# Moving the matmul operands' start addresses by 32, 96 and 128 bytes against the weights' in a two-layer hybrid trunk

## Chip, cores and metric

The kernel runs on one core of one Trainium2 chip. The metric is the device time of one execution in microseconds (us); lower is better. "Before" is the median of three runs.

## What is computed

Two residual layers over 512 tokens of width 1024, all in float32. Cut to what matters:

```python
for layer in range(2):
    xn = rmsnorm(h, norm_mix_g[layer])
    if layer % 2 == 0:      # S5 group + mLSTM group: one input projection, one output projection
        mix = s5_mlstm_mixer(xn, w_in, ..., w_q, w_k, ..., w_glu, w_out)
    else:                   # 16 query heads, 2 key/value heads, window 128
        mix = swa_sink_attention(xn, w_qkv, b_qkv, sinks, w_o, bias_band)
    h = h + mix
    gate, val = split(rmsnorm(h, norm_ffn_g[layer]) @ w_up)          # 1024 -> 2 x 2816
    h = h + (silu(causal_dwconv(gate, conv_w, conv_b)) * val) @ w_down   # 2816 -> 1024
return rmsnorm(h, norm_final_g)
```

## The kernel before

**Products.** Activations lie transposed: 128 channels on the partitions, the 512 tokens along the free dimension. A matmul's moving operand is one such block, 128 x 512, which is 2048 bytes in each partition; its stationary operand is a 128 x 128 block of weights, 512 bytes in each partition. Every float32 product is split into a high and a low part that are both float32r, and `block3` makes it of three matmuls: `whi` times the operand's high part (L1596), `whi` times its low part (L1597), `wlo` times its high part (L1598). Each of them has its own weight load.

**Weights.** SyncE streams the weights in tiles of 128 x 1024 through two buffers `raw`. ScalarE copies a tile to `whi` (L702), VectorE subtracts it to get `wlo` (L1057). Both are rings of 4 tiles of 4096 bytes, so that a weight block lies at a multiple of 512 bytes behind the start of `whi`.

**Operands.** Four pairs of tensors are the moving operands of the split products:

- `xhi`, `xlo`: the normed residual stream. Input projections, the feed-forward up projections (`product`), q/k/v of the attention, the S5 gate and the mixer's output projection.
- `ahi`, `alo`: 22 blocks of the gated feed-forward activation, used by the down projection (`down`). In layer 1 the last output tile is computed in two halves of 256 tokens.
- `xchi`, `xclo`: 4 blocks, from which q and k of the mLSTM are made (8 `block3`).
- `ohi`, `olo`: 8 blocks of the attention's output, used by its output projection (`wo_block`).

**Where they lie.** Offsets are per partition. `start_at(phase)` moves the next allocation up to a given phase in a line of `LINE` = 2048 bytes. `raw`, `whi`, `wlo`, `xhi`, `xlo` lie one behind the other and all start at phase 0. Behind them come constants (`con`, with the identity matrix; `mean_r`; `rstd`; `sq`; `ssum`; the parameters `prm`), and then, at `base`, a region that three layouts share, one after the other in time: the feed-forward's (`ahi`, `alo`, `gpad`, `cbuf`, `sbuf`, `vbuf`, `abuf`), the mixer's (`ff`, `gg`, `qT`, `kT`, `uc`, `uperm`, `xchi`, `xclo`, `sigo`, ...; `xin`, the input as loaded, lies in it too) and the attention's (`aq`, ..., `ohi`, `olo`, `st`). `plan` lays each out from `base`, sizes rounded up to 64 bytes, and moves `ohi` to `O_PHASE`. `A_PHASE` sets the phase of `base`. Up to `xchi` the mixer's layout has 65536 bytes, so `xchi` has the phase of `base`. `xc_at` is the same place as `xchi`, for tensors that take its room later: `m1re`, `m1im`, `vtok`, and behind `vtok` the buffer `wbuf` at `past_v` = `xc_at` + 8256. `h` lies at the end of the memory. With all phases 0, every moving operand of a `block3` starts at a multiple of 2048 bytes and every weight block at a multiple of 512.

**Other matmuls named below.** L1808 multiplies `vtok` (moving, 129 columns; a block lies 516 bytes behind the one before) with `wbuf` (stationary, slices of 512 bytes); it is in plain float32, of which the profile shows two instructions for each matmul. `qT` and `kT` are the operands of the mLSTM's scores (L1743), in plain float32 too.

Of the kernel before, what the change touches and what calls it, by code (L numbers as in the profile page):

```python
# [52 lines left out]
T_END = T_DN[1] + 3 * KB  # L53
assert T_WO + KB == T_UP[1] and T_END % 2 == 1

LINE, W_PHASE, X_PHASE, A_PHASE, O_PHASE = 2048, 0, 0, 0, 0
O_IN, O_O, O_GLU, O_OUT = 0, 12, 16, 20
O_UP = [28, 98]
O_DN = [O_UP[0] + 2 * FJ, O_UP[1] + 2 * FJ]
# [66 lines left out]
def build(nc, wstream, xT, params, bc, consts, band, outT, u_scratch):  # L126
# [9 lines left out]
    def at(name, shape, offset, dt=f32):  # L136
        return nc.alloc_sbuf_tensor_at(name, shape, dt, offset=offset)

    def size(shape):
        return (int(np.prod(shape[1:])) * 4 + 63) // 64 * 64  # L140
# [45 lines left out]
    def plan(*items, start=base):  # L186

        o, out = start, []
        for name, shape, dt in items:
            if name == "ohi":  # L190
                o += (O_PHASE - o) % LINE
            out.append(at(name, shape, o, dt))
            o += size(shape)
        assert o <= end, (items[0][0], o - end)
        return out


    h_at = end - size([P, KB, SEQ]) - (end - size([P, KB, SEQ])) % 64
    h = at("h", [P, KB, SEQ], h_at)
    ahi, alo, gpad, cbuf, sbuf, vbuf, abuf = plan(  # L200
        ("ahi", [P, FJ, SEQ], f32r), ("alo", [P, FJ, SEQ], f32r), ("gpad", [P, 2 + SEQ], f32),
        ("cbuf", [P, SEQ], f32), ("sbuf", [P, SEQ], f32), ("vbuf", [P, SEQ], f32), ("abuf", [P, SEQ], f32))
    assert base + 2 * size([P, FJ, SEQ]) + 5 * 2112 <= h_at

    F2 = [P, PAIRS, P]
    F4 = [P, 2, PAIRS, P]
    (ff, gg, qT, kT, uc, uperm, xchi, xclo, sigo, xs, ksb) = plan(
        ("ff", F4, f32), ("gg", F4, f32), ("qT", [P, HEADS, SEQ], f32), ("kT", [P, HEADS, SEQ], f32),
        ("uc", [P, GROUPS, NCH], f32), ("uperm", [P, 4, SEQ], f32),
# [2 lines left out]
    gg_at = base + size(F4)  # L212
    m1_at = base + 2 * size(F4)
    v_at = m1_at + 3 * 8192
    xc_at = v_at + 8192
    sigo_at = xc_at + 2 * 8192
    toep = at("toep", [P, CH, GROUPS, GCH], gg_at)
    gtmp = at("gtmp", [P, 2, PAIRS, GCH], base)
# [21 lines left out]

    tail = sigo_at + 8192 + size([P, 2, PAIRS, NCH]) + 2048
    bcp, xpad, cacc, xcf, ptmp, sm, qq, acol, turn, floor, hsm, selr = plan(
        ("bcp", [P, 4, PAIRS * GCH], f32), ("xpad", [P, 3 + SEQ], f32), ("cacc", [P, SEQ], f32),
        ("xcf", [P, SEQ], f32), ("ptmp", [P, 4, 256], f32), ("sm", [P, 40, PAIRS], f32),
# [1908 lines left out]
```

## Time and profile before

| | |
|---|---|
| median of three runs | 1069.69 us (1069.47 to 1070.51) |
| profiled execution | 1070.5 us, of it 1068.7 us span |
| granted TensorE clock | 0.998 of full speed, mean over the span |
| TensorE matmul busy | 1058.3 us (99%), 5552 instructions |
| TensorE weight load busy | 866.8 us (81%) |
| VectorE, ScalarE, GpSimd busy | 632.3 (59%), 464.6 (43%), 186.3 us (17%) |
| DMA | 107.27 MB, 29% of 16 engines' span |

The span goes from the first to the last instruction. The duration that the profile gives a matmul is from its start to its modelled end and overlaps the next one, so what a matmul costs in a dense stream is read from start to start, not from its duration.

### The profile page before, as it was taken

How to read it: one execution, taken by the hardware profiler on the slowest of the kernel's cores; microseconds unless marked ns; L12 is line 12 of the kernel's file. 1: busy time of each engine (PE TensorE's matmuls, PEld its weight loads, DVE VectorE, ACT ScalarE, POOL GpSimd, SP SyncE). 2: the span in 40 equal slices, each digit the busy share in tenths (PEclk: the TensorE clock that was granted, in tenths of full speed). 3: DMA queues.
4: the chain of work that ended last, by engine and by line, in shares of the span. 5: the costliest groups of instructions: out<-in, count | busy, mean ns of one | idle time of the engine just before them, and what ended most of it. 6: DMA issues, size and time to landing. Idle time of an engine off the chain costs nothing.

```text
span 1068.7 us, 15530 instructions
## 1 busy us (share of the span) xinstructions
PE 1058.3 (99%) x5552; PEld 866.8 (81%) x5552; DVE 632.3 (59%) x876; ACT 464.6 (43%) x733; POOL 186.3 (17%) x245
## 2 busy tenths in 40 slices
PE   9999999999999999999999999999999999999997
PEld 8787778888888888888888777888888888888886
DVE  6798755567666666633334774756666666643332
ACT  5455664544344444422323665554444444422221
POOL 8998911300000000000000221310000000000000
PEclk9999999999999999999999999999999999999999
DMA  6551025133222222323224111322222222222322
GB/s 231 168 128 40 15 91 197 59 119 118 94 89 92 98 98 98 98 99 118 98 102 144 61 60 41 118 94 100 85 99 93 98 98 98 98 99 99 119 79 79
DMA packets 36459, 107.27 MB, mean 100 GB/s; under 512 B 7808, under 2 KB 10112, under 8 KB 36160
## 3 DMA queue, kind: packets, MB, share of 16 engines
q1 hardware_dynamic: 36416, 106.69, 29.2%
q8 instruction: 28, 0.46, 0.2%
q14 instruction: 15, 0.12, 0.0%
HBM read 102.09 MB, written 3.15 MB: 98 GB/s over the span
## 4 chain that ended last, share of the span: by engine, by line
PE 93%; DVE 3%; ACT 1%; DMA 1%; SPq 1%; issue 1%; POOL 0%; DVEq 0%; ACTq 0%
PE bank L1596 29%; PE bank L1597 29%; PE bank L1598 29%; PE bank L1620 2%; DMA raw<-wstream 1%; PE bank L1986 1%; PE bank L1963 1%; PE bank L1743 1%; PE bank L1808 1%; DVE ssum L1090 0%; SPq L360 0%; PE bank L1707 0%; DVE wlo L1057 0%; DVE gtmp L1109 0%; PE bank L1687 0%
## 5 line engine op out<-in xcount | busy, mean ns | idle before, releaser
L1596 PE MATMUL bank<-xhi,whi 128*128 128x512 f32 x960 | 376.1, 392 | 0.8 <-DVE wlo L1057 0.6
L1597 PE MATMUL bank<-xlo,whi 128*128 128x512 f32 x960 | 373.7, 389 | 0.0
L1598 PE MATMUL bank<-xhi,wlo 128*128 128x512 f32 x960 | 373.6, 389 | 0.0
L1057 DVE TENSOR_TENSOR wlo<-raw,whi 128x1024 fp32r<-128x1024 f32 x177 | 226.0, 1278 | 205.4 <-ACT whi L702 204.8
L702 ACT ACTIVATE whi<-raw 128x1024 fp32r<-128x1024 f32 x177 | 187.1, 1058 | 323.2 <-PE bank L1598 301.0
L1596 PEld LDWEIGHTS bank<-xhi,whi 128*128 128x128 f32 x960 | 180.2, 188 | 40.6 <-DVE wlo L1057 1.0
L1598 PEld LDWEIGHTS bank<-xhi,wlo 128*128 128x128 f32 x960 | 180.2, 188 | 37.4
L1597 PEld LDWEIGHTS bank<-xlo,whi 128*128 128x128 f32 x960 | 180.3, 188 | 37.0 <-issue 0.2
L1596 PE MATMUL bank<-ahi,whi 128*128 128x512 f32 (+1 forms) x374 | 141.0, 377 | 0.0
L1598 PE MATMUL bank<-ahi,wlo 128*128 128x512 f32 (+1 forms) x374 | 140.8, 377 | 0.0
L1597 PE MATMUL bank<-alo,whi 128*128 128x512 f32 (+1 forms) x374 | 140.8, 377 | 0.0
L473 POOL COPY ssum<-sq 128x512 f32<-128x512 f32 x4 | 2.5, 614 | 554.9 <-ACT sq L708 554.9
L1596 PEld LDWEIGHTS bank<-ahi,whi 128*128 128x128 f32 x374 | 70.4, 188 | 13.0
L1598 PEld LDWEIGHTS bank<-ahi,wlo 128*128 128x128 f32 x374 | 70.4, 188 | 13.0
L1597 PEld LDWEIGHTS bank<-alo,whi 128*128 128x128 f32 x374 | 70.4, 188 | 12.7
L476 POOL TENSOR_TENSOR ssum<-ssum,sq 128x512 f32<-128x512 f32 x27 | 40.0, 1480 | 210.5 <-ACT sq L708 210.5
L973 ACT ACTIVATE ahi<-abuf 128x512 f32 x44 | 27.8, 632 | 72.5 <-DVE abuf L1430 72.5
L1432 DVE TENSOR_TENSOR alo<-abuf,ahi 128x512 f32 x44 | 30.5, 693 | 41.1 <-ACT ahi L973 41.1
L708 ACT ACTIVATE sq<-h 128x512 f32<-128x512 f32 (+1 forms) x31 | 19.4, 625 | 75.3 <-DVE h L1445 63.9
L1419 DVE SCALAR_TENSOR_TENSOR cbuf<-gpad,prm,cbuf 128x512 f32<-128x512 f32 x44 | 33.1, 752 | 6.7 <-DVE cbuf L1417 6.7
L1422 DVE SCALAR_TENSOR_TENSOR cbuf<-gpad,prm,cbuf 128x512 f32<-128x512 f32 x44 | 33.1, 752 | 6.7 <-DVE cbuf L1419 6.7
L1430 DVE TENSOR_TENSOR abuf<-vbuf,sbuf 128x512 f32<-128x512 f32 x44 | 30.5, 693 | 5.4
(264 smaller groups left out, 1052.1 us busy)
## 6 DMA issues: line engine op xcount, KB each, us to landing
raw<-wstream SPq DMA_DIRECT2D x177, 512.0 KB, 3.2
xin<-xT SPq DMA_DIRECT2D x8, 256.0 KB, 6.3
raw<-wstream SPq DMA_DIRECT2D x8, 256.0 KB, 5.6
h<-xT SPq DMA_DIRECT2D x1, 2048.0 KB, 8.4
u_scratch<-uperm SPq DMA_DIRECT2D x1, 1024.0 KB, 5.5
uc<-u_scratch SPq DMA_DIRECT2D x8, 128.0 KB, 4.5
bandsb<-band SPq DMA_DIRECT2D x1, 1024.0 KB, 4.8
outT<-outb SPq DMA_DIRECT2D x2, 512.0 KB, 2.8
```

Source lines behind the costliest of these rows:

```text
L476: G.tensor_tensor(ssum[:, :], ssum[:, :], sq[:, m % 2, :], ALU.add).then_inc(acc_done, 1)
L702: A(whi[:, t % RING, :], raw[:, t % RAWS, :], ACT.Copy).then_inc(hi_done, 1)
L973: A(ahi[:, i * 2 + jj, :], abuf[:, :], ACT.Copy).then_inc(ahi_done, 1)
L1057: V.tensor_tensor(wlo[:, t % RING, :], raw[:, t % RAWS, :], whi[:, t % RING, :].bitcast(f32), ALU.subtract).then_inc(lo_done, 1)
L1419: steps.up(V.scalar_tensor_tensor(out=cbuf[:, :], in0=gpad[:, 1:1 + SEQ], scalar=tap(1), in1=cbuf[:, :], op0=ALU.mult, op1=ALU.add))
L1422: V.scalar_tensor_tensor(out=cbuf[:, :], in0=gpad[:, 0:SEQ], scalar=tap(0), in1=cbuf[:, :], op0=ALU.mult, op1=ALU.add).then_inc(conv_done, 1)
L1430: V.tensor_tensor(abuf[:, :], vbuf[:, :], sbuf[:, :], ALU.mult).then_inc(a_done, 1)
L1432: V.tensor_tensor(alo[:, i * 2 + jj, :], abuf[:, :], ahi[:, i * 2 + jj, :].bitcast(f32), ALU.subtract).then_inc(alo_done, 1)
L1596: MM(dst, wh, rhi, start=start, stop=False)
L1597: MM(dst, wh, rlo, start=False, stop=False)
L1598: return MM(dst, wl, rhi, start=False, stop=stop)
L1620: return nc.tensor.transpose(dst, src, ident[0:k, 0:k])
```

## The change

The feed-forward's layout, and with it the whole shared region, starts at phase 32 instead of 0. In the mixer's layout 64 bytes more are left free ahead of `xchi`, so that `xchi` and `xclo` have phase 96. `ohi` and `olo` start at phase 128. `whi`, `wlo`, `xhi`, `xlo` and the constants stay where they are. No instruction is added, removed or moved.

```diff
-LINE, W_PHASE, X_PHASE, A_PHASE, O_PHASE = 2048, 0, 0, 0, 0
+LINE, W_PHASE, X_PHASE, A_PHASE, O_PHASE = 2048, 0, 0, 32, 128
+C_PAD = 64
...
         for name, shape, dt in items:
+            if name == "xchi":
+                o += C_PAD
             if name == "ohi":
                 o += (O_PHASE - o) % LINE
...
-    xc_at = v_at + 8192
+    xc_at = v_at + 8192 + C_PAD
```

## Rows read from the trace of the kernel before

**Rows 1.** The page, part 1: busy time and share of each engine.

```profile
PE 1058.3 (99%) x5552; PEld 866.8 (81%) x5552; DVE 632.3 (59%) x876; ACT 464.6 (43%) x733; POOL 186.3 (17%) x245
```

**Rows 2.** The page, part 4: chain that ended last, by engine.

```profile
PE 93%; DVE 3%; ACT 1%; DMA 1%; SPq 1%; issue 1%; POOL 0%; DVEq 0%; ACTq 0%
```

**Rows 3.** Groups by form, TensorE: xcount, busy us, mean ns.

```profile
L1596 PE MATMUL bank<-xhi,whi 128*128 128x512 f32 x960 | 376.1, 392 | 0.8 <-DVE wlo L1057 0.6 <-ACT ysb L862 0.2
L1596 PE MATMUL bank<-ahi,whi 128*128 128x512 f32 x330 | 128.4, 389 | 0.0
L1596 PE MATMUL bank<-ohi,whi 128*128 128x512 f32 x64 | 25.6, 400 | 0.0
L1596 PE MATMUL bank<-ahi,whi 128*128 128x256 f32 x44 | 12.6, 287 | 0.0
L1634 PE MATMUL bank<-xhi,whi 128*128 128x512 f32 x32 | 9.3, 414 | 0.0
L1596 PE MATMUL bank<-xchi,whi 128*128 128x512 f32 x8 | 3.1, 389 | 0.0
```

**Rows 4.** Timeline of TensorE, first and last starts of a down projection.

```profile
446.78 0.39 PE L1596 MATMUL bank<-ahi,whi 128*128 128x512 f32 x1
447.00 0.39 PE L1597 MATMUL bank<-alo,whi 128*128 128x512 f32 x1
447.23 0.39 PE L1598 MATMUL bank<-ahi,wlo 128*128 128x512 f32 x1
...
566.46 0.39 PE L1596 MATMUL bank<-xhi,whi 128*128 128x512 f32 x1
```

**Rows 5.** Windows, TensorE: us, busy (instructions), clock, DMA share, GB/s.

```profile
300.00:400.00 100.00, 100.00 (x443) 1.00 0.27 94
450.00:550.00 100.00, 100.00 (x443) 1.00 0.30 105
```

**Rows 6.** Timeline of weight loads, around 500 us.

```profile
499.82 0.19 PEld L1597 LDWEIGHTS bank<-alo,whi 128*128 128x128 f32 x1
500.05 0.19 PEld L1598 LDWEIGHTS bank<-ahi,wlo 128*128 128x128 f32 x1
```

**Rows 7.** Chain, 1050 to 1054.2 us, the half-width matmuls.

```profile
1050.10 0.12 PE bank L1598
...
1054.06 0.12 PE bank L1598
```

**Rows 8.** Timeline of TensorE, plain float32 matmuls of the mixer.

```profile
122.65 0.61 PE L1808 MATMUL bank<-vtok,wbuf 128*128 128x129 f32 x4
...
127.97 0.61 PE L1808 MATMUL bank<-vtok,wbuf 128*128 128x129 f32 x4
...
133.42 0.61 PE L1808 MATMUL bank<-vtok,wbuf 128*128 128x129 f32 x4
```

**Rows 9.** One line's instructions, L1808: duration ns min/median/max, first and last start us.

```profile
L1808 PE MATMUL bank<-vtok,wbuf x80: 273/275/378, 119.7 to 139.7; 128*128 128x129 f32 x80
```

**Rows 10.** Waits of TensorE, whole span: us, times, longest.

```profile
PE bank L1624 <- POOL mean_r L459: 1.2, 1, 1.2
PE bank L1596 <- DVE wlo L1057: 0.6, 1, 0.6
```

**Rows 11.** Windows of the two down projections, all engines (columns: PE, PEld, DVE, ACT, POOL).

```profile
446.80:566.40 119.60, 119.60 (x529) 99.09 (x528) 43.48 (x42) 34.58 (x40) 8.41 (x7) 1.00 0.30 104
938.90:1054.40 115.50, 115.50 (x554) 97.49 (x553) 37.80 (x40) 28.90 (x32) 8.39 (x7) 1.00 0.25 87
```

**Rows 12.** The page, part 6: the input's load, KB each, us to landing.

```profile
xin<-xT SPq DMA_DIRECT2D x8, 256.0 KB, 6.3
raw<-wstream SPq DMA_DIRECT2D x8, 256.0 KB, 5.6
```

## The prediction, made before the changed kernel was run

> **What bounds the kernel.** I read the page first. TensorE is busy 99% of the span [rows 1] and holds 93% of the chain that ended last [rows 2]; the waits that the trace finds for it in the whole span are 1.8 us in their two largest [rows 10]. So the time is the number of matmuls times what each takes from start to start, and only a change of that spacing can move it by much. Durations don't show it, because they overlap (389 ns and more [rows 3]), so I went to the timeline. The down projection of layer 0 starts at 446.78 us, and the first matmul behind it at 566.46 [rows 4]: 119.68 us for 8 x 22 x 3 = 528 matmuls, or 226.7 ns each. The reader should see that nothing else happens there: VectorE is busy 43.5 of 119.6 us, and TensorE all of it [rows 11]. The stage that reads `xhi` and `xlo` runs at the same pace, 443 matmuls in 100 us as against 443 [rows 5].
>
> Of the 226.7 ns, 512 / 2.4 = 213.3 are columns at the granted clock of 1.00 (the 2.4 GHz level). 13.3 ns are left over. The half-width matmuls tell what kind of cost this is. From 1050.10 to 1054.06 us the chain has 33 steps [rows 7], so 120.0 ns each; 256 columns are 106.7, and again 13.3 are left. The difference of the two spacings, 106.7 ns for 256 columns, is exactly the columns' own time. The excess does not grow with the moving operand that is read; it comes once per matmul. What also comes once per matmul is the load of the next weights, issued in the shadow of the matmul: the loads start 0.23 us apart and take 0.19 [rows 6].
>
> **The change part by part.** It adds no instruction. It shifts moving operands against weights that stay. By the counts [rows 3], each times three for L1596 to L1598: `ahi`/`alo` 330 x 3 = 990 full and 44 x 3 = 132 half matmuls, by 32 bytes; `xchi`/`xclo` 8 x 3 = 24, by 96; `ohi`/`olo` 64 x 3 = 192, by 128. Together 1338. The (960 + 32) x 3 = 2976 matmuls of `xhi`/`xlo` keep both addresses and should keep 226.7 ns. All that counts is what the shift does to the 13.3 ns of 1338 matmuls. Every `block3` of before has the same relative phase (both starts are multiples of 512), so the trace does not show another one in float32r. I bound it from both sides.
>
> *Best case.* All 13.3 ns are a collision of the two reads and go: 1338 x 13.3 = 17.8 us saved. The nearest row for what stays is a plain float32 matmul, in which a column takes two cycles and two reads have more room: L1808, four of 129 columns in 0.61 us, the last of them of 0.275 (the median) [rows 8, 9]. (0.61 - 0.275) / 3 = 112 ns from start to start, of which 129 x 2 / 2.4 = 107.5 are columns: some 4 ns left over. By that the gain is 1338 x (13.3 - 4.2) = 12.2 us.
>
> *Worst case.* The collision of reads doubles: 13.3 ns more, 17.8 us.
>
> *Nothing.* Two things in the trace speak for it. First, the 13.3 ns are 32 cycles at 2.4 GHz, at either width. The moving operand passes 2048 bytes in 213 ns while a weight block of 512 bytes passes in less than 190, so the distance between the two addresses runs through hundreds of bytes in every matmul. If only certain distances collided, part of the load would be hit and part not; a shift of the start by 32 to 128 bytes would then move where it is hit and hardly how often. Second, there is one place where the relative phase does vary. L1808 reads `vtok` in blocks 516 bytes apart against `wbuf`. At the third block of heads 0, 1 and 2 the moving operand starts 8, 24 and 40 bytes behind a multiple of 512, and the weights 64 behind one. All three groups take 0.61 us for four [rows 8], so relative starts of -56, -40 and -24 bytes cost the same 4 ns. This is at half the column rate, so it can hide a collision; it is still the nearest row, and I take 0 from it.
>
> The Trainium skill ("TensorE: Matmul & The Clock Gate", section "Wait — 56ns, not 53.3ns?") gives a warm back-to-back spacing of N / 2.4 + about 2.5 ns; the row of 226.7 ns is 10.9 above the 215.8 of that rule, so rule and row differ here. An estimate by that page, had the change removed all 10.9 ns from 1338 matmuls, would be 14.6 us less. Against that stands "SBUF — State Buffer", section "Who interferes with whom": TensorE has two independent read ports, one for the moving operand and one for weight loads, and waits on no one. By this rule no phase matters. No row of before decides between them.
>
> *The rest of the region.* With `base`, the operands of VectorE, ScalarE and GpSimd in the three layouts move by 32 or 96 bytes, still multiples of 32. Their durations may change by little; in the down projections they lie under TensorE, which is busy throughout [rows 11], and a slower `gpad` or `cbuf` step would have to use up the idle 41% of VectorE [rows 1]. Operands that share the region keep their distance from each other: `qT` and `kT`, `vtok` and `wbuf`. The tail reads `h`, `ssum`, `sq` and writes where `xhi` lies; none moves. The input's load writes at phase 32 instead of 0: 6.3 us to land against 5.6 of the weight pieces beside it [rows 12]. A tenth of that would be 0.6 us at the start, which is inside what can be told. I take 0.
>
> **Sum.** Profiled execution 1070.5 us (span 1068.7 and 1.8 around it) + 0. It lies 0.8 above the median of three, so the forecast on the median's side is 1069.7 us.
>
> **Rivals.**
>
> *Slower: the shifted start costs read slots.* Place: the 1338 matmuls, above all the two down projections. If a moving operand that starts off the weights' phase is fetched in more pieces, or meets each weight read where it now just passes it, the spacing goes up. Doubling the excess gives 240.0 and 133.3 ns and 1069.7 + 17.8 = 1087.5 us. It decides (over 0.2%, or 2.1 us) from 2.1 / 1338 = 1.6 ns on, which is 4 cycles. For it: the excess is a whole number of cycles per matmul in every stage, at every weight block, and what all of these share is exactly phase 0; so phase 0 could be the good case. Against it: L1808.
>
> *Faster: phase 0 is the bad case.* The two reads start together (a load of this stage every 0.23 us, as the matmuls [rows 4, 6]) at the same place in a line, and a shift takes them apart. 1069.7 - 12.2 = 1057.5 us, at most 1051.9. For it: an excess that appears in full-rate matmuls and nearly not in half-rate ones is what a shared resource looks like. Against it: the sweep of distances, and a shared resource need not know addresses.
>
> *The three shifts differ,* for instance 32 bytes cost and 128 do not. Then 1122 of 1338 matmuls follow the 32, and the sum is within a fifth of one of the cases above. It belongs to their chances.
>
> **How the numbers follow.** No change 0.46, slower 0.35, faster 0.19. Within 0.2% is about what a measurement of this kernel can tell from no change. The forecast is 1069.7 us. For the likeliest case alone the range is 1068 to 1072. The range of 8 in 10 takes in that case and the slower one up to its bound, 1087.5, and of the faster one only the small part down to 1065 (under 4 ns per matmul). It leaves out most of the faster case and losses beyond a doubling.
>
> **What would show it.** The start-to-start of `ahi`/`alo` in the down projection (now 226.7, and 120.0 at half width), of `ohi`/`olo` and of `xchi`/`xclo`, beside that of `xhi`/`xlo`, which must stay 226.7. If the first three are 226.7, the forecast holds. If they differ, the count times the difference is the whole change of the time. I am wrong if the full-rate read does see the phase, which the half-rate rows of L1808 can't exclude.

## The result: 0.7% slower, all of it in the spacing of the shifted matmuls

| | before | after |
|---|---|---|
| median | 1069.76 us (4 runs, 1069.47 to 1070.51) | 1077.09 us (4 runs, 1076.91 to 1077.38) |
| ratio | | 1.0066, 95% interval 1.0055 to 1.0078 |
| span of the profiled execution | 1068.7 us | 1075.3 us |
| instructions | 15530 | 15530 |

The change costs 7.3 us. The forecast of no change failed; the range of 1065 to 1087.5 held the time only because it took in the rival "slower", which had a chance of 0.35.

The page after, busy time by engine, answers to [rows 1]:

```profile
PE 1065.1 (99%) x5552; PEld 865.7 (81%) x5552; DVE 631.1 (59%) x876; ACT 464.7 (43%) x733; POOL 185.0 (17%) x245
```

TensorE is busy 6.8 us longer with the same 5552 matmuls; ScalarE moves by 0.1 us, and the others are busy 1.1 to 1.3 us less. Windows of TensorE after (us, busy, instructions, clock), the same two as in [rows 5]:

```profile
300.00:400.00 100.00, 100.00 (x443) 1.00 0.29 94
450.00:550.00 100.00, 100.00 (x430) 1.00 0.31 105
```

The up projection reads `xhi`/`xlo`, which did not move, and still gets 443 matmuls into 100 us. The down projection reads `ahi`/`alo` and gets 430 where it had 443, at the same granted clock of 1.00. The timeline of TensorE after, first and last start of that stage, as in [rows 4]:

```profile
446.21 0.40 PE L1599 MATMUL bank<-ahi,whi 128*128 128x512 f32 x1
446.45 0.39 PE L1600 MATMUL bank<-alo,whi 128*128 128x512 f32 x1
...
569.42 0.40 PE L1599 MATMUL bank<-xhi,whi 128*128 128x512 f32 x1
```

(569.42 - 446.21) / 528 = 233.35 ns, against 226.7. The half-width matmuls go the other way. Chain after, start and length, first and last of 30 steps, as in [rows 7]:

```profile
1057.21 0.12 PE bank L1600
...
1060.72 0.12 PE bank L1600
```

3.51 us / 30 = 117.0 ns, where it was 120.0. Over all 129 gaps inside the two halves the means are 116.7 and 119.9 (two more gaps, of 0.8 and 0.3 us, have other matmuls in them and are left out). Timeline after, attention output projection and q/k:

```profile
675.25 0.39 PE L1600 MATMUL bank<-olo,whi 128*128 128x512 f32 x1
...
702.90 0.39 PE L1599 MATMUL bank<-xhi,whi 128*128 128x512 f32 x1
```

```profile
72.83 0.40 PE L1599 MATMUL bank<-xchi,whi 128*128 128x512 f32 x1
...
78.44 0.40 PE L1599 MATMUL bank<-xhi,whi 128*128 128x512 f32 x1
```

119 matmuls of `ohi`/`olo` at 128 bytes take 232.4 ns each (before, the same stretch had 27.00 us, 226.9 ns). 24 of `xchi`/`xclo` at 96 bytes take 233.8. The sum: 990 x 6.67 - 132 x 3.2 + 192 x 5.5 + 24 x 7.1 = 6.6 - 0.4 + 1.1 + 0.2 = 7.4 us, for 7.3 measured. (The other 72 matmuls of `ohi`/`olo` stand in short runs of 12 to 15 between other work; from the first to the last of all 192, 0.9 us were added.) Nothing that a median could show is left over for other engines. The input's load lands in 5.8 us where it took 6.3 [rows 12]:

```profile
xin<-xT SPq DMA_DIRECT2D x8, 256.0 KB, 5.8
```

### The profile page after: what moved, and what is told of

The parts are those of the page before. It is cut to its first block, busy times and chain, and to the rows that moved or that the text cites. A ratio compares the mean times of both kernels' runs of the same rounds, so it can differ in the third digit from the quotient of the medians.

```text
span 1075.3 us, 15530 instructions
## 1 busy us (share of the span) xinstructions
PE 1065.1 (99%) x5552; PEld 865.7 (81%) x5552; DVE 631.1 (59%) x876; ACT 464.7 (43%) x733; POOL 185.0 (17%) x245
## 4 chain that ended last, share of the span: by engine, by line
PE 95%; DVE 2%; ACT 1%; DMA 1%; SPq 1%; issue 1%; POOL 0%; DVEq 0%; ACTq 0%
PE bank L1599 30%; PE bank L1601 29%; PE bank L1600 29%; PE bank L1623 2%; PE bank L1989 1%; PE bank L1966 1%; DMA raw<-wstream 1%; PE bank L1746 1%; PE bank L1811 1%; DVE ssum L1093 0%; PE bank L1710 0%; SPq L363 0%; PE bank L1690 0%; DVE wlo L1060 0%; PE bank L1774 0%
```

## The experiments

Theory R: what counts is the distance between the moving operand and the weights that are loaded under it. Theory M: what counts is the moving operand's own start. Two more questions came with them: over which period the distance counts, and whether any distance is better than 0.

### Both moved together, and the weights alone

```diff
-LINE, W_PHASE, X_PHASE, A_PHASE, O_PHASE = 2048, 0, 0, 0, 0
+LINE, W_PHASE, X_PHASE, A_PHASE, O_PHASE = 2048, 32, 32, 32, 32     # all32
+LINE, W_PHASE, X_PHASE, A_PHASE, O_PHASE = 512, 32, 0, 0, 0         # w32
```

> Kernel before, with the weights, xhi/xlo, ahi/alo, xchi/xclo and ohi/olo all at phase 32. Theory R (only the distance between moving operand and weights counts): distances are 0 as before, so 226.7 ns everywhere and 1069.7 us within 2. Theory M (the moving operand's own start counts, for instance that it is off a multiple of 64 bytes): all 4182 full-width split matmuls take the 233.3 ns that ahi/alo took at 32, +27.9 us, the 132 half ones 3.2 ns less, -0.4: 1097 us.

> Kernel before, with whi/wlo alone at phase 32 and every moving operand at a multiple of 512 bytes (the line is set to 512 bytes instead of 2048, for room). Distance moving minus weights -32 in all 4182 full-width split matmuls. Theory R: the spacing leaves 226.7 ns everywhere; if -32 costs what +32 did, 233.3 ns and 1097 us. Theory M: all moving operands are still aligned, 226.7 ns and 1069.7 us.

Measured: all32 1070.3 us, ratio 1.0005 (0.9996 to 1.0015). w32 1095.28 us, ratio 1.0240 (1.0223 to 1.0257). Windows of TensorE, all32 and then w32:

```profile
300.00:400.00 100.00, 100.00 (x443) 1.00 0.27 94
450.00:550.00 100.00, 100.00 (x443) 1.00 0.31 105
```

```profile
300.00:400.00 100.00, 100.00 (x430) 1.00 0.27 92
450.00:550.00 100.00, 100.00 (x430) 1.00 0.30 103
```

Theory R holds and M falls: with everything at 32 the spacing is what it was at 0, and with the weights alone at 32 both stages have 430 in 100 us, although no moving operand is off its line. w32 is 25.8 us slower, where 27.3 were expected (1097 against 1069.7). In the two feed-forward layers the spacing is the expected 233.3. What is missing lies in part where split products come in short runs: in the attention's items (583.5 to 671.7 us before, 597.1 to 686.1 in w32) 241 of them stand between other matmuls, and 0.9 us were added where 241 x 6.67 ns would be 1.6. Another part lies at the start, where the 98 split matmuls of the first 30 us added nothing. Why this is so was not followed further.

### A map of TensorE alone

These kernels leave out both layers. They load the input, copy it into two float32r buffers and run only matmuls, 24 in a row for each entry of a list:

```python
for n, (wp, mp, cols) in enumerate(PLAN):       # start of weights and operand in bytes, columns
    m = mall[:, mp // 4:mp // 4 + cols]
    dst = bank[n % 8]
    for b in range(8):
        for j, hl in enumerate((0, 0, 1)):      # high, high, low weights
            ins = MM(dst[:, 0:cols], weights(wp, hl, b), m, start=b == 0 and j == 0,
                     stop=b == 7 and j == 2)
```

The product is not the kernel's; each map was run once, and only its spacing is read. "Distance" is the start of the moving operand minus the start of the weights.

> TensorE alone, no other work of the layers: 24 matmuls of 128x512 float32r (the order of the weights as in the split product: block b high, high, low) for each distance of the moving operand from the weights, 0 to 512 bytes in steps of 16, then 544, 1024, 1056, 2048, 2080, 4, 8 and 36. Theory R with banks: 226.7 at 0, 233.3 at 32, about 232 at 96 and 128, and a map that repeats with some period that is at most 512 (blocks 512 bytes apart all gave 226.7); some distance may lie under 226.7. Theory M: a map in the moving start alone, looking the same in this kernel; the two are told apart by the next kernel. If neither engine but TensorE is needed for the cost, the numbers of the changed kernel come back here.

> As the map, in this order: 256 columns at distances 0 to 512 in steps of 32 (120.0 at 0, 116.8 at 32 expected); 128 columns at 0, 32, 64, 96, 128, 256; then 512 columns with weights and moving operand moved together by 32, 64, 96, 128, 256 (theory R: 226.7 each; theory M: as the map at 32, 64, ...); then the weights alone moved by 32, 64, 96, 128, 256 (R: a map of the negative distances; M: 226.7 each); then (weights, moving) = (32,0), (32,64), (32,96), (64,32), (64,96), (64,128): R gives equal spacings for equal differences, M for equal moving starts.

Timeline of the first map. A row is one entry, so the next row's start minus its own, over 24, is the spacing. The rows are distances 16, 32, 48, (...), 240, 256, 272:

```profile
33.65 5.72 PE L54 MATMUL oddd<-mall,wall 128*128 128x512 f32 x24
39.21 5.77 PE L54 MATMUL evene<-mall,wall 128*128 128x512 f32 x24
44.81 5.76 PE L54 MATMUL oddf<-mall,wall 128*128 128x512 f32 x24
...
111.81 5.61 PE L54 MATMUL oddb<-mall,wall 128*128 128x512 f32 x24
117.26 5.64 PE L54 MATMUL evenc<-mall,wall 128*128 128x512 f32 x24
122.74 5.72 PE L54 MATMUL oddd<-mall,wall 128*128 128x512 f32 x24
```

231.7 ns at 16, 233.3 at 32, 227.1 at 240 (its first matmul still 234). With the first matmuls after each change left out (how many shifts some entries by a few tenths, because the gaps repeat in groups of unequal ones):

| distance | 0 | 16 | 32 | 48 | 64 | 80 | 96 | 112 |
|---|---|---|---|---|---|---|---|---|
| ns | 226.7 | 231.8 | 233.3 | 233.3 | 229.3 | 231.1 | 233.9 | 231.1 |

| distance | 128 | 144 | 160 | 176 | 192 | 208 | 224 | 240 |
|---|---|---|---|---|---|---|---|---|
| ns | 232.4 | 233.2 | 233.9 | 233.1 | 233.2 | 234.8 | 233.2 | 226.7 |

256 to 496 give the same values again to 0.1 ns. 1024 and 2048 give those of 0, and 1056 and 2080 those of 32. So the period is 256 bytes. The three numbers of the changed kernel (233.35, 233.8, 232.4 at 32, 96, 128) are in the table, with VectorE, ScalarE and the weight stream silent: they have no share in the cost.

The second map says that only the difference counts, sign included. Weights and operand together at 32 to 256 settle at 226.7. The weights alone at 32, which is distance -32 or 224, give 233.2, and (weights, operand) = (32, 64) gives 233.4 like 32. For 256 columns the order is another: 120.0 at 0, 117.8 at 32, and 113.3 at 192, the lowest.

At 128 columns the distance hardly matters (111.6 to 111.8). Two rows of the second map's timeline, 128 columns at distances 64 and 96; 2.68 us / 24 is 111.7 ns, where 128 / 2.4 = 53.3 are columns:

```profile
82.84 2.84 PE L56 MATMUL oddf<-mall,wall 128*128 128x128 f32 x24
85.52 2.85 PE L56 MATMUL eveng<-mall,wall 128*128 128x128 f32 x24
```

240 columns, in the third map, take no more (112.2 at 0, 111.8 at 192). So at these widths something other than the columns sets the pace; each matmul's weight load is one candidate, which no run here tested. This matters for the prediction's row of L1808: it has 129 columns and 112 ns, and beside it even float32r of 128 columns shows no effect of the distance.

### Parts of the change in the kernel

```diff
+LINE, W_PHASE, X_PHASE, A_PHASE, O_PHASE = 2048, 0, 0, 32, 0        # ff32,  C_PAD = 224
+LINE, W_PHASE, X_PHASE, A_PHASE, O_PHASE = 2048, 0, 0, 192, 0       # ff192, C_PAD = 64
+LINE, W_PHASE, X_PHASE, A_PHASE, O_PHASE = 2048, 0, 256, 768, 1280  # off256, no C_PAD
```

> The feed-forward part of the change alone: ahi/alo at phase 32, ohi/olo back at 0, xchi/xclo at 256 (pad 224 instead of 64). By the distances modulo 256 bytes: 990 matmuls at 233.3 ns instead of 226.7 (+6.6 us), 132 half ones at 116.8 instead of 120.0 (-0.4), q/k and attention output at 226.7: +6.2 us, 1075.7. If the region's other tenants (VectorE's buffers, the input's load) had a share in the 7.3 us, it would come out elsewhere, because they move with the base here too.

> ahi/alo at phase 192, xchi/xclo at 256, ohi/olo at 0. By the map of TensorE alone: full matmuls 233.2 ns (+6.5 us for 990), half ones 113.3 instead of 120.0 (-0.9 us for 132): +5.6 us, 1075.2. A theory in which what counts is only how far the start is from the weights' (further is worse) would have it slower than at 32.

> Weights at 0, xhi/xlo at 256, ahi/alo (and xchi/xclo) at 768, ohi/olo at 1280: three starts that are all multiples of 256 and no two alike in 2048. Period of 256 bytes: 226.7 ns everywhere after a few matmuls at each change of operand, 1069.7 us within 2. If only a full match in the 2048-byte line were good: up to 1097.

Measured, against 1069.90 of before: ff32 1075.96 us (ratio 1.0057, 1.0043 to 1.0071), ff192 1075.52 (1.0053, 1.0039 to 1.0067), off256 1069.79 (1.0001, 0.9992 to 1.0010). All three lie within 0.4 us of what the map gives. Windows of TensorE in ff32, and in off256:

```profile
300.00:400.00 100.00, 100.00 (x443) 1.00 0.29 94
450.00:550.00 100.00, 100.00 (x430) 1.00 0.32 105
```

```profile
300.00:400.00 100.00, 100.00 (x443) 1.00 0.28 94
450.00:550.00 100.00, 100.00 (x443) 1.00 0.31 106
```

The feed-forward part carries 6.1 of the 7.3 us. off256 shows the period in the whole kernel. In ff192 the half-width matmuls have the 113 ns of the map. Its chain, start of the first and the last of 35 steps:

```profile
1049.94 0.11 PE bank L1599
...
1053.91 0.11 PE bank L1601
```

### Which read, and is there a better distance

The third to fifth map take a distance for each of the high and low parts, and can read one column again and again (stride 0) instead of walking:

```python
if kind == "one weight column":
    w = w[:, 0:1].to_broadcast([P, P])
if kind == "one moving column":
    m = m[:, 0:1].to_broadcast([P, cols])
```

> TensorE alone again, in this order: 512 columns at distances 228, 232, 236, 240, 244, 248, 252 (the flat place may be a narrow one, from 240 to 256); 256 columns at 176, 184, 192, 200, 208, 240; 384 columns at 0, 32, 192, 240; 240 columns at 0, 272 at 192, 240 at 192, 272 at 0; then unlike distances for the high and low operand or the high and low weights; then, with one weight column read 128 times (stride 0), distances 0 and 32, and the same with one moving column read 512 times; last 0 and 32 as a check. If the excess of 13.3 ns is a collision of the weight read with the moving read in the memory, it goes (to about 216 ns or less) or loses its dependence on the distance when either read stays in one place. If it is a fixed cost of changing weights, it stays 226.7 at 0.

Timeline of the third map: one weight column at 32, one moving column at 0 and at 32, then a plain 0 and 32:

```profile
163.58 5.73 PE L69 MATMUL evena<-mall,wall 128*128 128x512 f32 x24
169.15 5.41 PE L69 MATMUL oddb<-mall,wall 128*128 128x512 f32 x24
174.40 5.41 PE L69 MATMUL evenc<-mall,wall 128*128 128x512 f32 x24
179.64 5.60 PE L69 MATMUL oddd<-mall,wall 128*128 128x512 f32 x24
185.08 5.77 PE L69 MATMUL evene<-mall,wall 128*128 128x512 f32 x24
```

With the moving read held in place the spacing is 218.7 ns (5.25 us / 24) at either distance: 8.0 ns less than the best walking case, and no dependence on the distance. With the weight read held in place it is 231.6 at 0 and 232.0 at 32: the dependence all but goes too, but the cost stays. So at the two distances tried the dependence needs both reads to walk. That fits a collision of two reads in the memory, and does not show one. If a read held in place changes nothing else, at most 5.3 of the 13.3 ns are a fixed cost of each matmul. The expectation had both cases fall to about 216, or lose their dependence: both lost it, and only the moving one came near 216.

384 columns gave 173.3 at 32 and at 192 and settled there at 0 too, 13.3 over the columns' 160, but 180.0 at 240. So of the four distances tried at 384 columns only 0 has the same excess at 256, 384 and 512 columns (13.3 ns). At 192 it is 6.6, 13.3 and 19.9 ns and grows with the width. The third map's eight entries with unlike distances for the high and the low part gave 230.9 to 234.9.

> TensorE alone, 512 columns, distances from 256 down to 4 in steps of 4, then 240, 0, 240, 224, 240. Two questions. Is there any distance under 226.7 ns? Theory S (the spacing is bound from below by 13.3 ns of excess for 512 columns): none. Theory G (a gap between the read streams fits somewhere, as 192 does for 256 columns at 113.3): one with 220 or so. And does the spacing hang on what ran just before? 240 gave 226.7 behind 224 in the first map and 236.8 behind 236 in the third: if the history decides, it differs again here between 244, 0 and 224 as forerunners; if one of the two readings came from something else, it is the same each time.

> TensorE alone, 512 columns, distance of the high operand from the high weights 0 throughout, the low weights at w and the low operand at m, w and m from 0 to 224 in steps of 32, m fastest; last 256 columns at 192, 0, 192. Theory S: no pair under 226.7 ns, (0, 0) the best. Theory G: some pair under it. At 256 columns 113.3 at 192 and 120.0 at 0.

Of the 64 distances in steps of 4, none is under 226.7. Seven besides 0 reach it (28, 60, 92, 108, 156, 236, 252); the worst is 240.1 at 244. None of the 64 pairs of the fifth map is under 226.7. Besides (0, 0) only (low weights, low operand) = (128, 160) comes to it, after its first eight matmuls; the others average 228.9 to 234.1. For the full width theory S holds as far as this was searched, but 0 is the lowest value together with others, not alone.

The history counts. Timeline of the fourth map, distances 244, 240, 236 near its start, and at its end 240 (behind 4), 0, 240, 224:

```profile
44.93 5.91 PE L63 MATMUL oddf<-mall,wall 128*128 128x512 f32 x24
50.68 5.84 PE L63 MATMUL eveng<-mall,wall 128*128 128x512 f32 x24
56.35 5.61 PE L63 MATMUL oddh<-mall,wall 128*128 128x512 f32 x24
61.80 5.76 PE L63 MATMUL evena<-mall,wall 128*128 128x512 f32 x24
...
385.93 5.60 PE L63 MATMUL evenc<-mall,wall 128*128 128x512 f32 x24
391.38 5.64 PE L63 MATMUL oddd<-mall,wall 128*128 128x512 f32 x24
396.85 5.76 PE L63 MATMUL evene<-mall,wall 128*128 128x512 f32 x24
402.45 5.76 PE L63 MATMUL oddf<-mall,wall 128*128 128x512 f32 x24
```

At 240 bytes the same 24 matmuls take 236.3 ns each behind 244, 227.1 behind 4 and 233.3 behind 0. The same operand addresses have several steady patterns, and what ran before picks one. The distance just before does not settle it: behind 224, the entry at 240 took 226.7 in the first map and 233.3 at the end of the fourth. In the fifth map the 256-column entry at 192 took 117.8 the first time (behind 512-column entries) and 113.3 the second.

### The version that the maps point to

Full-width matmuls stay at 0. Only the last output tile, in two halves of 256 columns, gets distance 192, by putting its weight tiles elsewhere in the ring:

```diff
+SHIFT = {T_END - 3: (-48, 8 * P), T_END - 2: (-48, 7 * P), T_END - 1: (16, 7 * P), T_END - 4: (0, 7 * P)}
...
-            A(whi[:, t % RING, :], raw[:, t % RAWS, :], ACT.Copy).then_inc(hi_done, 1)
+            dst, n = place(whi, t, i, per)
+            A(dst, raw[:, t % RAWS, 0:n], ACT.Copy).then_inc(hi_done, 1)
```

(elements of 4 bytes, and how many are copied; `wlo` and `block3` follow.)

> Kernel before (all phases 0), but the weight tiles of the last output tile, the one in two halves of 256 columns, are written 192 bytes ahead of their place in the ring (the last of the three 64 bytes behind), so that the 132 half-width matmuls run at distance 192 modulo 256. By the map 113.3 ns instead of 120.0 if they fall into the pattern that ff192 showed: -0.9 us, 1068.9, all of it after about 1045 us. If they fall into the other one (117.8, as the first group at 192 in the fifth map): -0.3 us. All full-width matmuls stay at 226.7. Either is at the edge of what five rounds tell; the spacing tells it.

Measured: 1068.84 us against 1069.60, ratio 0.9995 (0.9986 to 1.0004). Chain of half192, first and last of 16 steps:

```profile
1045.06 0.12 PE bank L1611
...
1046.94 0.12 PE bank L1609
```

117.5 ns each, the pattern of 117.8, and it holds for the first 90 of the 132 matmuls: the whole first half and the first weight tile of the second. Then come other matmuls (L1946, L1948), and the 42 behind them, on the other two tiles, settle in the other pattern. Later in the same chain, first and last of 22 steps:

```profile
1055.46 0.11 PE bank L1611
...
1057.95 0.11 PE bank L1609
```

2.49 us / 22 = 113.2 ns. So both patterns occur in one kernel, at the same distance and with the same tiles (the second and third had the slower pattern in the first half), and the result lies between the two cases that were expected. What differs is what ran before. The first pattern is entered from a stream at distance 0; ff192, which enters from one at 192, has 113.5 throughout. Over the 129 gaps inside the two halves the mean is 116.5, against 119.9, and the trace's gain 132 x 3.4 = 0.45 us. The median is 0.8 lower than before's, which no interval here can tell from nothing. No version clearly beats before.

## What the prediction had right and wrong, point by point

**What bounds the kernel** was right, and so was the place of the change: 1338 matmuls, their start-to-start, nothing else. The 2976 untouched ones kept 226.7 ns. The region's other tenants and the input's load cost nothing that shows. The reading that the excess "comes once per matmul" holds at distance 0, where 256, 384 and 512 columns all have 13.3 ns; at 192 it grows with the width.

**The step that failed is "I take 0 from it".** It had two supports. The first was the sweep argument, that the distance runs through hundreds of bytes in every matmul, so that a shift moves where a collision falls and hardly how often. The map refutes it: in steps of 16 bytes the spacing goes from 226.7 to 234.8 and repeats every 256. The two streams don't slide past each other at random; they fall into a repeating pattern (231, 235, 234, 234 ns in turn in the changed down projection), and which pattern depends on the starting distance, down to 4 bytes. The second was L1808, distances of -56, -40 and -24 bytes without a cost. Modulo 256 these are 200, 216 and 232, where float32r matmuls of 512 columns take 233.3, 234.1 and 233.3 ns. The row was read rightly, but it is of 129 columns and plain float32. The prediction said that the half column rate could hide a collision and then still went by the row. The map shows that the width alone would have hidden it: at 128 columns float32r has 111.6 to 111.8 ns at every distance tried. Whether plain float32 at full width sees the distance, no run here shows.

**The rival "slower"** had the right place and direction. Of its two forms, the one in which the distance to the weight read counts is the right one (all32 and w32 rule out the moving start alone), and it had the right hint: what all stages share is exactly phase 0. Its size was off. It priced a doubling of the excess, 13.3 ns; 5.5 to 7.1 came, so 7.3 us instead of 17.8. The deciding point of 1.6 ns per matmul was passed by a factor of four. It missed that the half-width matmuls would gain. That the time lies in the stated range is owed to this rival's upper bound, a doubling taken from no row, and so is luck as far as the forecast goes.

**The rival "faster"** was half right in kind: a part of the 13.3 ns hangs on the moving read (8.0 of it goes with that read held in place). But 0 is one of the good cases of those tried, not the bad one. Its objection that a shared resource need not know addresses fails: the cost does hang on them.

**The rule of two independent read ports** (the Trainium skill, "SBUF — State Buffer", section "Who interferes with whom") makes no difference between phases, and so spoke for no change. The runs of this case disagree: with TensorE alone at work, the distance of its two reads changes the spacing by up to 13 ns. The other rule that was weighed, N / 2.4 + about 2.5 ns (the Trainium skill, "TensorE: Matmul & The Clock Gate", section "Wait — 56ns, not 53.3ns?"), gives 215.8 at 512 columns. The nearest that any dense stream of 512 columns in the maps came to it was 218.7, with the moving read held in place.

**What stays open.** What lies behind the 256 bytes, what sets the pace at 128 and 240 columns, and why some distances settle in two or three different patterns, no run here settles. A collision in the memory was argued from the cases with a read held in place; it was not seen itself.

## What to carry to other kernels

In a stream of float32r matmuls, each with its own weight load, put moving operands and weight blocks at equal addresses modulo 256 bytes; 32 bytes off cost 3% of each 512-column matmul here. The page hardly shows it: TensorE is 99% busy in both, and the mean duration of the group of `ahi` is 382 ns instead of 377. The matmul count in a window shows it plainly. Where an excess per matmul is the same everywhere in a trace and all addresses share one phase, the trace can't say what another phase does: that uniformity is a reason to widen the range upward, not to take zero. A row of another width and dtype is weak support: check first that the effect could show in it at all.

## What the runs showed that was not expected

- The spacing of 512-column float32r matmuls takes preferred values, besides others between them: 226.7 and 233.3 ns, and 240.0 at the worst, which are 544, 560 and 576 cycles at 2.4 GHz; at 256 columns 113.3 and 120.0, 272 and 288 cycles.
- At 256 columns the best distance (192, 113.3 ns) is one of the bad ones at 512 columns (233.2).
- The same matmuls at the same addresses have more than one steady spacing (236.3, 233.3 and 227.1 ns at 240 bytes), chosen by what ran before. After a change of operand the stream needs from none to about eight matmuls to settle.
- A weight read of one column, which one would take for the lightest, was slower (231.6 ns) than an ordinary one at distance 0 (226.7).
- Float32r matmuls with a weight load each have nearly the same spacing at 128 and at 240 columns (111.7 and 112.2 ns at distance 0).
